# A hybrid decoder layer on one core: sliding-window units inside the input panels, operands stacked as high and low part

## The chip, the core and the metric

The kernel runs on one core of a Trainium2 chip. Its engines work side by side and meet only through semaphores: PE (TensorE) multiplies into PSUM, DVE (VectorE) and ACT (ScalarE) read PSUM and SBUF, POOL (GpSimd) reads SBUF, SP (SyncE) issues DMAs. Each engine runs its own instructions in program order. The metric is the device time of one execution in microseconds (us), lower is better.

## The reference, cut to what matters

One decoder layer, 512 tokens, width 2048, all in float32. A norm, one input projection whose columns feed two head groups, attention in both, an output projection, a norm, a gated FFN.

```python
proj = h @ w_in[layer]
c_q, c_kv, k_r, sq, sk, sv = jnp.split(proj, split_idx, axis=-1)   # 512, 512, 64, 1024, 128, 128
...
out_a = mla_attention(q, k_a, v_a)          # 8 heads, dense causal, latents c_q and c_kv
out_b = swa_attention(sq..., sk..., sv..., sinks[layer], rel_bias)
```

and of the sliding group, 16 heads of 64, in two groups of 8 that share a key and a value head:

```python
s = jnp.einsum('bnqhgd,bnkhd->bnhgqk', qb, kb) * scale     # 128 queries against 256 keys
s = jnp.where(valid, s + bias, NEG_INF)
m = jnp.maximum(jnp.max(s, axis=-1, keepdims=True), sink)
p = jnp.exp(s - m)
probs = p / (jnp.sum(p, axis=-1, keepdims=True) + jnp.exp(sink - m))
out = jnp.einsum('bnhgqk,bnkhd->bnqhgd', probs, vb)
```

## The kernel before

Every float32 product is made of three matmuls in the faster fp32r format: each operand is split into a high part (ACT's copy, rounded) and a low part (DVE's subtraction), and `three` (L722) sums high x high, high x low and low x high.

**Input panels.** The 1088 + 1280 columns of w_in are 19 panels of 128 columns, q = 0 to 18: four of c_kv, four of c_q, the rotary key, the sliding keys, the sliding values, and eight of sliding queries (q = 11 to 18). SP fetches a panel into `raw[q % 2]` (`fetch`, L733), 1 MB, when the low part of panel q-2 is written (`lo_ready`). ACT makes the high part of panel q+2 when PE has finished panel q (`used`), DVE the low part (`split_hi` L453, `split_lo` L465). PE runs 16 x 3 matmuls of 512 columns for a panel (L2426). DVE takes the result out of PSUM with the norm's factor (`take`, L1720; semaphore `taken`). ACT's and DVE's loops over the panels (L1122, L1710) hold, in this order for each q: units if there are any, the take, the splits for q+2.

**Sliding units.** A unit is one group of four heads (gh) and one block of 128 queries (n): 16 units, u = 4 gh + n. With n = 0 there is no earlier block of keys, so it has half the keys. A pipeline step `window(s)`, written once for each engine, holds: PE (L2377) the scores of unit s, the transposes of the probabilities of unit s-3, the values of unit s-4; DVE (L1669) bias and maxima of unit s (L1680), the reciprocal of s-1, the low half of the transposed probabilities of s-3 (L1698); ACT (L1083) the high half of s-3, the four exponentials of s (L1106), in their middle the copy of values s-4 to `mix_s` (L1091); POOL the scaling by the reciprocal (L974). Steps 0 and 1 stand in panel 17, steps 2 to 19 after the panels; the first product of the next stage (`rotary_queries`, `queries`) is woven into steps 17 to 19.

For the scores two heads of 64 lie on 128 partitions; the keys are padded with zeros (`kpad`) so that each of the two sees only its own 64 rows. A full unit has two `three` of 512 columns, one with n = 0 two of 256. For the values `vpad` is padded likewise, and a full unit has four `three` of 256 columns, one with n = 0 two.

**After the units.** Four pairs of dense heads. `keys_of`, `values_of`, `scores` (L2479 to L2516) of a pair need the split w_uq and w_ukv panels (q = 19, 20 and so on), and `keys_of` writes to bank 0 when DVE has copied the rotary queries from it (`r_in`, L1816). Then the output projection and the FFN, which fill the rest of the span.

The order on every engine is written out by hand in these loops.

## Time and profile before

| | |
|---|---|
| median of 3 runs | 1902.78 us (1902.52 to 1903.36) |
| the profiled execution | 1902.99 us |
| its span | 1901.2 us |
| PE busy | 1874.4 us |
| DVE busy | 1511.3 us |
| ACT busy | 915.2 us |
| POOL busy | 63.1 us |

The median is over runs without the profiler. The span is from the first to the last instruction of the profiled execution. Matmuls are pipelined: a record of one lasts longer than the distance to the next, so the time of a stream is read from starts. Times in the rows are from the span's start. An idle time that a row names is that of the engine just before the instruction, and the arrow says what ended it.

### The profile page before, as it was taken

The page shows a single profiled execution, that of the slowest core. Times are in us where ns is not written, and L with a number is a line of the kernel's source. Part 1 is how long each engine was busy: PE and PEld are TensorE (multiplying, and loading weights), DVE is VectorE, ACT ScalarE, POOL GpSimd, SP SyncE. Part 2 cuts the span into 40 slices and gives each one's busy share as a digit, 9 for nine tenths or more (in the row PEclk, how much of TensorE's full clock was granted, in tenths as well). Part 3 has the DMA queues.
Part 4 walks back from the last instruction along what each step waited for, and adds up shares of the span by engine and source line. Part 5 has one row for each costly group of instructions (what it writes and reads, how often), then busy time and mean ns, then how long its engine had stood idle before and what let it go on. Part 6 is the DMA issues. An engine that isn't in the chain of part 4 may idle for free.

```text
span 1901.2 us, 22151 instructions
## 1 busy us (share of the span) xinstructions
PE 1874.4 (99%) x8726; PEld 1556.3 (82%) x8726; DVE 1511.3 (79%) x1608; ACT 915.2 (48%) x1222; POOL 63.1 (3%) x63
## 2 busy tenths in 40 slices
PE   9999999999999999999999999999999999999998
PEld 7788788888888788888888888888888788888886
DVE  4863486775557988888888888889898988888888
ACT  5331484564465655454554554555455743333332
POOL 1210141000000000000000000000000000000000
PEclk9999999999999999999999999999999999999999
DMA  7444202137675437254272452734626865646563
GB/s 215 139 114 120 80 13 89 52 118 259 230 268 192 112 111 252 80 178 159 96 255 89 166 183 91 236 102 153 198 92 242 313 242 219 227 160 258 218 224 130
DMA packets 206197, 317.18 MB, mean 167 GB/s; under 512 B 9972, under 2 KB 143181, under 8 KB 199949
## 3 DMA queue, kind: packets, MB, share of 16 engines
q1 hardware_dynamic: 202128, 305.69, 47.1%
q10 hardware_dynamic: 3036, 6.66, 1.1%
q0 software_dynamic: 928, 3.41, 0.8%
q8 instruction: 69, 1.13, 0.2%
q14 instruction: 36, 0.29, 0.0%
HBM read 262.49 MB, written 52.98 MB: 166 GB/s over the span
## 4 chain that ended last, share of the span: by engine, by line
PE 61%; DVE 3%; issue 1%; DMA 1%; ACT 0%; DVEq 0%; ACTq 0%
PE pair L2664 13%; PE pair L2666 13%; PE pair L2665 13%; PE pair L2713 6%; PE pair L2714 6%; PE pair L2715 6%; PE pair L2675 1%; PE pair L2734 1%; PE pair L2732 1%; PE pair L2733 1%; DVE unit_lo L1923 1%; DMA w_b<-in_w_down 1%; DVE ring_lo L2172 0%; DMA h_forms<-h_stage 0%; ACT unit_hi L1339 0%
## 5 line engine op out<-in xcount | busy, mean ns | idle before, releaser
L2664 PE MATMUL pair<-unit_hi,xf_hi 128*128 128x512 f32 x1224 | 481.3, 393 | 6.6 <-DVE unit_lo L1923 6.6
L2666 PE MATMUL pair<-unit_hi,xf_lo 128*128 128x512 f32 x1224 | 476.9, 390 | 0.0
L2665 PE MATMUL pair<-unit_lo,xf_hi 128*128 128x512 f32 x1224 | 476.4, 389 | 0.0
L2664 PEld LDWEIGHTS pair<-unit_hi,xf_hi 128*128 128x128 f32 x1224 | 229.9, 188 | 55.5 <-issue 5.8
L2666 PEld LDWEIGHTS pair<-unit_hi,xf_lo 128*128 128x128 f32 x1224 | 229.8, 188 | 48.5
L2665 PEld LDWEIGHTS pair<-unit_lo,xf_hi 128*128 128x128 f32 x1224 | 230.0, 188 | 46.4
L469 DVE TENSOR_TENSOR wlo<-raw,whi 128x2048 fp32r<-128x2048 f32 (+2 forms) x59 | 124.1, 2110 | 93.1 <-ACT whi L462 93.0
L2713 PE MATMUL pair<-ring_hi,hfs 128*128 128x512 f32 x480 | 187.4, 390 | 1.5 <-ACT ht L1363 0.8
L2714 PE MATMUL pair<-ring_lo,hfs 128*128 128x512 f32 x480 | 186.8, 389 | 0.0
L2715 PE MATMUL pair<-ring_hi,hfs 128*128 128x512 f32 x480 | 186.8, 389 | 0.0
L462 ACT ACTIVATE whi<-raw 128x2048 fp32r<-128x2048 f32 (+2 forms) x60 | 105.0, 1757 | 146.2 <-PE pair L726 141.2
L1482 ACT ACTIVATE ring_hi<-w_b 128x2048 fp32r<-128x2048 f32 (+1 forms) x55 | 95.9, 1760 | 120.9 <-DVE w_b L2152 53.9
L2172 DVE TENSOR_TENSOR ring_lo<-w_b,ring_hi 128x2048 fp32r<-128x2048 f32 (+1 forms) x55 | 115.0, 2090 | 4.7 <-ACT ring_hi L1482 4.6
L724 PE MATMUL pair<-act_hi,whi 128*128 128x512 f32 x288 | 114.6, 398 | 3.1 <-DVE wlo L1606 2.3
L725 PE MATMUL pair<-act_lo,whi 128*128 128x512 f32 x288 | 112.2, 390 | 0.0
L726 PE MATMUL pair<-act_hi,wlo 128*128 128x512 f32 x288 | 112.2, 390 | 0.0
L2184 DVE TENSOR_TENSOR y<-y,pair 128x1024 f32<-128x1024 f32 x63 | 76.6, 1215 | 43.4 <-PE pair L2715 43.4
L2713 PEld LDWEIGHTS pair<-ring_hi,hfs 128*128 128x128 f32 x480 | 90.1, 188 | 21.7 <-DVE ring_lo L2172 2.2
L2715 PEld LDWEIGHTS pair<-ring_hi,hfs 128*128 128x128 f32 x480 | 90.1, 188 | 18.9
L2714 PEld LDWEIGHTS pair<-ring_lo,hfs 128*128 128x128 f32 x480 | 90.1, 188 | 18.5
L724 PE MATMUL pair<-whi,mixt 128*128 128x512 f32 x256 | 100.1, 391 | 0.1
L726 PE MATMUL pair<-whi,mixt 128*128 128x512 f32 x256 | 99.6, 389 | 0.0
(392 smaller groups left out, 3427.9 us busy)
## 6 DMA issues: line engine op xcount, KB each, us to landing
w_b<-in_w_down SPq DMA_DIRECT2D x40, 1024.0 KB, 5.1
h_forms<-h_stage SPq DMA_DIRECT2D x71, 512.0 KB, 4.9
raw<-in_w_o SPq DMA_DIRECT2D x32, 1024.0 KB, 5.0
hfs<-h_forms SPq DMA_DIRECT2D x30, 1024.0 KB, 8.1
raw<-in_w_in SPq DMA_DIRECT2D x16, 1024.0 KB, 6.0
w1a<-in_w_gate SPq DMA_DIRECT2D x16, 512.0 KB, 3.7
w1a<-in_w_up SPq DMA_DIRECT2D x16, 512.0 KB, 5.9
w1b<-in_w_gate SPq DMA_DIRECT2D x16, 512.0 KB, 3.9
```

Source lines behind the costliest of these rows:

```text
L462: last = nc.scalar.activation(dst, src, ACT.Copy)
L469: last = nc.vector.tensor_tensor(dst, src, f(hi), ALU.subtract)
L724: nc.tensor.matmul(out_ap, a[0], b[0], start=first, stop=False)
L725: nc.tensor.matmul(out_ap, a[0], b[1], start=False, stop=False)
L726: return nc.tensor.matmul(out_ap, a[1], b[0], start=False, stop=last)
L2172: nc.vector.tensor_tensor(ring(ring_lo, n), weights_form(f_, np_), f(ring(ring_hi, n)), ALU.subtract).then_inc(d_lo, 1)
L2664: nc.tensor.matmul(dst, a[0], w[0], start=(at, k) == (0, 0), stop=False)
L2665: nc.tensor.matmul(dst, a[0], w[1], start=False, stop=False)
L2666: last = nc.tensor.matmul(dst, a[1], w[0], start=False, stop=(at, k) == (3, 1))
L2713: nc.tensor.matmul(dst, a[0], b[0], start=k == 0, stop=False)
L2714: nc.tensor.matmul(dst, a[0], b[1], start=False, stop=False)
L2715: last = nc.tensor.matmul(dst, a[1], b[0], start=False, stop=k == np_ - 1)
```

## The change

- The sliding queries, keys and values are no longer padded. A query operand `sq_parts` holds for each head its high part on 64 partitions and its low part on the other 64; `sk_parts` holds the high part (and, in a second tile, the low part) of the keys on both halves. A unit's scores are, for each of its four heads, two matmuls of 256 columns (128 with n = 0) that contract over 128 partitions.
- The values are stacked along the output: `sv_parts` has 64 columns of high and 64 of low part, so a value matmul has 512 columns and its result has high x probabilities on partitions 0 to 63 and low x probabilities on 64 to 127. There are four such matmuls for a unit (two with n = 0). ACT copies the lower 64 partitions to `pv_low` and DVE adds both into `mix_s` (`value_add`), where ACT alone copied before. DVE does the addition of unit s-5 at the head of step s; the next unit's values wait for it (`s_out`).
- Steps 0 to 11 run inside panels 13 to 18, two in each: on PE after the 8th and the 14th of a panel's 16 chunks, on ACT and DVE at the head of the panel's turn. These steps use one pair of banks for scores, so the scores of s wait for the maxima of s-1. Steps 12 to 19 follow the panels.
- The queries are split panel by panel, as soon as a panel is taken, and only two panels of them are held.
- To make room, the low part of panels 12 to 20 is written over the raw panel (`low_part`, `in_place`), and the fetch of panel q then waits for `used` of panel q-2. The first w_uq panel comes in four pieces.
- Bank numbers, addresses, the place of the rotary key's parts and what the third w_o panel's fetch waits for change with it. POOL no longer zeroes `kpad` and `vpad`.

```diff
+        def in_place(q):
+            return Q_SQ + 1 <= q <= Q_UKV
+        def low_part(q):
+            return wlo_raw[q % 2] if in_place(q) else wlo[q % 2]
...
             def fetch(q, src, view):
-                if q >= 2:
+                if in_place(q - 2):
+                    sp_.wait_ge(used, q - 1)
+                elif q >= 2:
                     sp_.wait_ge(lo_ready, q - 1)
...
                 if i == 2:
-                    sp_.wait_ge(act_l, N_ROTATED)
+                    sp_.wait_ge(act_l, N_KG2)
...  (ACT)
+            def split_queries_hi(j):
+                act.wait_ge(taken, Q_SQ + j + 1)
+                if j >= 4:
+                    act.wait_ge(s_qk, 4 * (j // 2 - 1))
+                for e in range(2):
+                    rows = slice(64 * e, 64 * e + 64)
+                    last = nc.scalar.activation(sq_parts[j // 2 % 2][rows, 2 * (j % 2) + e, :], sq[j % 2][rows, :],
+                                                ACT.Copy)
+                last.then_inc(q_hi, 1)
...
                         act.wait_ge(s_pv, u + 1)
-                        nc.scalar.activation(mix_s[:, 2 * gh:2 * gh + 2, P * n:P * n + P],
-                                             bank[7][:, 0:256].rearrange("p (c n) -> p c n", c=2),
-                                             ACT.Copy).then_inc(s_out, 1)
+                        if u:
+                            act.wait_ge(s_out, u)
+                        nc.scalar.activation(pv_low[0:64, :], bank[7][64:128, :], ACT.Copy).then_inc(s_low, 1)
...
-                if q == N_IN - 2:
-                    window(0)
-                    window(1)
+                for s in panel_windows(q):
+                    window(s)
+                if what == "sq":
+                    split_queries_hi(j)
                 if 0 < q < N_IN - 1:
                     split_hi(q + 2, q % 2)
...  (DVE)
+            def value_add(u):
+                gh, _, n, _ = unit(u)
+                dve.wait_ge(s_low, u + 1)
+                for e in range(2):
+                    high, low = (t[0:64, 256 * e:256 * e + 256].rearrange("p (c n) -> p c n", c=2)
+                                 for t in (bank[7], pv_low))
+                    c0 = 2 * (gh % 2)
+                    last = nc.vector.tensor_tensor(mix_s[gh // 2][64 * e:64 * e + 64, c0:c0 + 2, P * n:P * n + P],
+                                                   high, low, ALU.add)
+                last.then_inc(s_out, 1)
...
             def window(s):
+                if s >= 5:
+                    value_add(s - 5)
...
-                    take(sq[:, j, :]).then_inc(taken, 1)
+                    take(sq[j % 2][:, :]).then_inc(taken, 1)
+                    split_queries_lo(j)
                 if 0 < q < N_IN - 1:
                     split_lo(q + 2, q % 2)
...
-            for s in range(2, UNITS + 3):
+            for s in range(FIRST_LATE, UNITS + 4):
                 window(s)
                 if s == UNITS + 1:
                     dve.wait_ge(ukv_hi, 1)
                     first_values_lo(0)
-            dve.wait_ge(hi_ready, Q_UKV + 1)
-            first_values_lo(1)
+                if s == UNITS + 2:
+                    dve.wait_ge(hi_ready, Q_UKV + 1)
+                    first_values_lo(1)
+            value_add(UNITS - 1)
...  (PE)
-                    if s == 1:
-                        pe.wait_ge(taken, N_IN - 2)
-                    if s >= 2:
-                        pe.wait_ge(s_max, s - 1)
+                    if s == FIRST_LATE:
+                        pe.wait_ge(taken, N_IN)
+                    elif s:
+                        pe.wait_ge(s_max, s if s < FIRST_LATE else s - 1)
                     keys = slice(P * n - P + lo, P * n + P)
-                    for cc in range(2):
-                        dst = bank[(s + 1) % 2 * 2 + cc].rearrange("p (e k) -> p e k", e=2)[:, :, lo:256]
-                        last = three(dst, [qs[gh % 2][i][:, cc, P * n:P * n + P] for i in range(2)],
-                                     [kpad[i][:, g, :, keys] for i in range(2)], True, True)
+                    for hd in range(4):
+                        dst = score_bank(s, hd).rearrange("p (e k) -> p e k", e=2)[:, hd % 2, lo:256]
+                        q_both = sq_parts[gh % 2][:, hd, P * n:P * n + P]
+                        nc.tensor.matmul(dst, q_both, sk_parts[0][:, g, keys], start=True, stop=False)
+                        last = nc.tensor.matmul(dst, q_both, sk_parts[1][:, g, keys], start=False, stop=True)
...
-                    parts = [(kb, e, h) for kb, h in halves(u) for e in range(2)]
-                    for m, (kb, e, h) in enumerate(parts):
+                    parts = [(kb, h, i) for kb, h in halves(u) for i in range(2)]
+                    for m, (kb, h, i) in enumerate(parts):
                         pe.wait_ge(s_lo, h + 1)
-                        c0 = 64 - 64 * e
-                        last = three(bank[7][:, 0:256], ...
+                        last = nc.tensor.matmul(bank[7], sv_parts[:, n - 1 + kb, g, :], spt[u % 2][i][:, kb, :],
+                                                start=m == 0, stop=m == len(parts) - 1)
...
-                    if q == N_IN - 2 and k == 7:
-                        window(1)
+                    if q >= Q_UNITS and k in (7, 13):
+                        window(panel_windows(q)[k // 13])
```

Here `Q_SQ` is 11, `Q_UNITS` 13, `Q_UKV` 20, `FIRST_LATE` 12.

## Rows read from the trace of the kernel before

**Rows 1.** The page, parts 1 and 2: busy time by engine; granted clock in 40 slices.

```profile
PE 1874.4 (99%) x8726; PEld 1556.3 (82%) x8726; DVE 1511.3 (79%) x1608; ACT 915.2 (48%) x1222; POOL 63.1 (3%) x63
...
PEclk9999999999999999999999999999999999999999
```

**Rows 2.** Windows: length; busy us of PE, PEld, DVE, ACT, POOL; clock; DMA share, GB/s.

```profile
159.15:227.89 68.74, 68.74 (x307) 57.03 (x306) 22.86 (x41) 18.16 (x30) 2.93 (x2) 1.00 0.34 92
227.89:276.62 48.73, 44.41 (x308) 39.45 (x307) 45.18 (x194) 44.30 (x164) 21.89 (x13) 1.00 0.12 33
276.62:290.92 14.30, 14.30 (x91) 12.71 (x90) 7.26 (x11) 6.17 (x14) 2.58 (x3) 1.00 0.04 3
```

**Rows 3.** Waits of PE, whole trace: us in total, times, longest.

```profile
PE pair L724 <- DVE wlo L1606: 2.3, 1, 2.3
...
PE pair L724 <- ACT mix_s L1091: 2.1, 5, 0.7
```

**Rows 4.** Timeline of PE: start us, us, line, out<-in, count.

```profile
236.14 1.03 PE L2407 MATMUL pair<-ident,sp 128*128 128x128 f32 x8
237.01 0.39 PE L724 MATMUL pair<-spt_hi,vpad_hi 128*128 128x256 f32 x1
237.23 0.28 PE L725 MATMUL pair<-spt_lo,vpad_hi 128*128 128x256 f32 x1
237.35 0.29 PE L726 MATMUL pair<-spt_hi,vpad_lo 128*128 128x256 f32 x1
```

**Rows 5.** Timeline of DVE and ACT behind panels 14 and 15.

```profile
181.11 0.69 DVE L1722 TENSOR_TENSOR sq<-pair,rrow 128x512 f32<-128x512 f32 x1 [6.58 <-PE pair L726]
...
191.99 0.69 DVE L1722 TENSOR_TENSOR sq<-pair,rrow 128x512 f32<-128x512 f32 x1 [6.58 <-PE pair L726]
...
192.05 1.92 ACT L462 ACTIVATE whi<-raw 128x2048 fp32r<-128x2048 f32 x1 [8.96 <-PE pair L726]
...
194.00 2.29 DVE L469 TENSOR_TENSOR wlo<-raw,whi 128x2048 fp32r<-128x2048 f32 x1 [1.32 <-ACT whi L462]
...
196.21 1.29 DVE L1661 TENSOR_TENSOR qs_lo<-sq,qs_hi 128x512 fp32r<-128x512 f32 x2
```

**Rows 6.** DMA issues from 165, 181 and 190 us: size, us from issue to landing.

```profile
raw<-in_w_in SPq DMA_DIRECT2D x1, 1024.0 KB, 5.7
...
raw<-in_w_in SPq DMA_DIRECT2D x1, 1024.0 KB, 6.9
...
raw<-in_w_uq SPq DMA_DIRECT2D x1, 768.0 KB, 4.7
```

**Rows 7.** Timeline of DVE among the units.

```profile
229.03 0.42 DVE L1680 CUSTOM_DVE_ANT_0 sp<-pair,bias 128x256 f32<-128x256 f32 x1
...
229.37 0.42 DVE L1680 CUSTOM_DVE_ANT_0 sp<-pair,bias 128x256 f32<-128x256 f32 x1
...
230.80 0.42 DVE L1680 CUSTOM_DVE_ANT_0 sp<-pair,bias 128x256 f32<-128x256 f32 x1
...
235.69 1.26 DVE L1698 TENSOR_TENSOR spt_lo<-pair,spt_hi 128x512 fp32r<-128x512 f32 x2
...
236.87 0.41 DVE L1680 CUSTOM_DVE_ANT_0 sp<-pair,bias 128x256 f32<-128x256 f32 x1
```

**Rows 8.** Timeline of DVE: four operations on 64 partitions.

```profile
131.58 2.78 DVE L1722 TENSOR_TENSOR skd<-pair,rrow 64x512 f32<-64x512 f32 x4
```

**Rows 9.** Timeline of ACT among the units.

```profile
227.15 1.15 ACT L1067 ACTIVATE qs_hi<-sq 128x512 fp32r<-128x512 f32 x2 [9.66 <-PE pair L726]
...
238.24 1.07 ACT L1081 ACTIVATE spt_hi<-pair 128x512 fp32r<-128x512 f32 x2
...
239.19 0.52 ACT L1106 ACTIVATE sp<-sp,st 128x256 f32<-128x256 f32 x1
...
240.18 0.38 ACT L1091 ACTIVATE mix_s<-pair 128x256 f32<-128x256 f32 x1
```

**Rows 10.** Timeline of DVE and PE before the keys.

```profile
289.44 0.69 DVE L1816 COPY t_sb<-pair 128x512 f32<-128x512 f32 x1
...
290.92 0.40 PE L724 MATMUL pair<-ckv_hi,whi 128*128 128x512 f32 x1
```

More of the change, by code:

```diff
@@ L67 @@
 Q_KR = [what for what, _, _ in IN_PANELS].index("kr")
+Q_SQ = [what for what, _, _ in IN_PANELS].index("sq")
+Q_UNITS = Q_SQ + 2
 PAIRS = MLA_HEADS // 2
@@ L137, in build @@
         wlo = [sb(f"wlo{i}", 32 + 8 * i, [P, 2048], F32R) for i in range(2)]
+        wlo_raw = [sb(f"wlo_raw{i}", 8 * i, [P, 2048], F32R) for i in range(2)]
         ident = sb("ident", 220, [P, P])
@@ L489, in half_bank @@
         def half_bank(h):
-            return bank[4 + h % 3]
+            return bank[4 + (h + 1) % 3]
         def value_bank(h):
@@ L754, in _ @@
                 q = Q_MLA + 2 * p
-                fetch(q, wuq_v[:, :, 384 * p:384 * p + 384], k4(raw[q % 2], 384))
+                if p == 0:
+                    first = k4(raw[q % 2], 384)
+                    for c0, w, a in ((192, 128, 128), (NOPE, ROPE, 256), (192 + NOPE, ROPE, 320), (0, 128, 0)):
+                        if a == 128:
+                            fetch(q, wuq_v[:, :, c0:c0 + w], first[:, :, a:a + w])
+                        else:
+                            sp_.dma_start(first[:, :, a:a + w], wuq_v[:, :, c0:c0 + w]).then_inc(uq_in, 16)
+                else:
+                    fetch(q, wuq_v[:, :, 384 * p:384 * p + 384], k4(raw[q % 2], 384))
                 fetch(q + 1, wukv_v[:, :, 512 * p:512 * p + 512], k4(raw[(q + 1) % 2]))
@@ L948, in _ @@
             pool.wait_ge(made, 7)
-            for t in (*kpad, vpad[0]):
-                make(nc.gpsimd.memset(f(t[:]), 0.0))
             for latent in range(2):
@@ L1153, in _ @@
                 if what == "sk":
-                    act.wait_ge(made, 11)
                     act.wait_ge(taken, q + 1)
-                    for i in range(4):
-                        g, e = i // 2, i % 2
-                        rows = slice(64 * e, 64 * e + 64)
-                        copy_hi(kpad[0][rows, g, e, :], skd[rows, g, :])
-                if q == N_IN - 4:
-                    act.wait_ge(taken, N_IN - 6)
-                    split_queries_hi(0, 0)
-                    split_queries_hi(0, 1)
+                    copy_hi(sk_parts[0][:, :, :], skd[:, :, :])
                 if what == "sv":
                     act.wait_ge(r_done, 1)
-                    copy_hi(kr[0][:, :], kr_a[:, :])
+                    copy_hi(kr[0][:, :], kraw[:, :])
                 if q == N_IN - 8:
                     act.wait_ge(sv_t, 1)
-                    copy_hi(vpad[0][:, :, :, 64:128], bank[4].rearrange("p (b g d) -> p b g d", b=TB, g=2))
+                    copy_hi(sv_parts[:, :, :, 0:64], bank[4].rearrange("p (b g d) -> p b g d", b=TB, g=2))
             act.wait_ge(used, N_IN)
-            load_band(1)
-            split_queries_hi(1, 0)
-            split_queries_hi(1, 1)
-            transposed_out(0)
-            for s in range(2, UNITS + 4):
+            for s in range(FIRST_LATE, UNITS + 4):
                 window(s)
@@ L1657, in latent_norm, with split_queries_lo @@
                     sub_lo((ckv, cq)[n][1][:, i, :], craw[n][:, i, :], (ckv, cq)[n][0][:, i, :])
-            def split_queries_lo(gh, half):
-                dve.wait_ge(q_hi, 2 * gh + half + 1)
-                nc.vector.tensor_tensor(qs[gh % 2][1][:, half, :], sq[:, 2 * gh + half, :],
-                                        f(qs[gh % 2][0][:, half, :]), ALU.subtract).then_inc(q_lo, 1)
+            def split_queries_lo(j):
+                dve.wait_ge(q_hi, j + 1)
+                for e in range(2):
+                    rows, other = slice(64 * e, 64 * e + 64), slice(64 - 64 * e, 128 - 64 * e)
+                    part = sq_parts[j // 2 % 2][:, 2 * (j % 2) + e, :]
+                    last = nc.vector.tensor_tensor(part[other, :], sq[j % 2][rows, :], f(part[rows, :]),
+                                                   ALU.subtract)
+                last.then_inc(q_lo, 1)
+            def value_add(u):
+                gh, _, n, _ = unit(u)
+                dve.wait_ge(s_low, u + 1)
+                for e in range(2):
+                    high, low = (t[0:64, 256 * e:256 * e + 256].rearrange("p (c n) -> p c n", c=2)
[4 more added lines that the diff above has]
+                last.then_inc(s_out, 1)
             def reciprocal_of(u):
@@ L1678, in window @@
                     for hd in range(4):
-                        scores = bank[(s + 1) % 2 * 2 + hd // 2].rearrange("p (e k) -> p e k", e=2)[:, hd % 2, lo:256]
+                        scores = score_bank(s, hd).rearrange("p (e k) -> p e k", e=2)[:, hd % 2, lo:256]
                         last = nc.vector.tensor_tensor_reduce(
@@ L2568, in out_products @@
                 last.then_inc(used, 1)
-            for s in range(2, UNITS + 4):
+            for s in range(FIRST_LATE, UNITS + 4):
                 if s == UNITS + 1:
```

119 lines of the change are left out of this document (53 added, 66 removed).

## The prediction, made before the changed kernel was seen

> **What bounds the kernel now.** I read the page first. PE is busy for 99% of the span and its granted clock is at the upper level, 2.4 GHz, in every slice [rows 1] (1.00 in the stretches of [rows 2]), so the end is moved only by PE: by matmuls taken out, or by waits put in or taken out. The profiled execution took 1902.99 us, 1.79 us more than its span, and lies 0.2 us above the median of 1902.78. I work against 1902.99.
>
> Then the stretches [rows 2]. Input panels 13 to 18 run from 159.15 to 227.89 with PE never idle: 68.74 us, in which units 0 and 1 compute their scores. The other units follow alone, 227.89 to 276.62, where DVE is busy for 45.2 of 48.7 us, ACT for 44.3 and PE idles for 4.3; its waits there are short, the five for ACT's copy of the values 0.7 us at most [rows 3]. The last units' values are mixed with the first query products until the keys start at 290.92. So panels plus units take 131.77 us. Outside the panels DVE and ACT are as full as PE; inside them they are nearly empty. What is moved goes from the one place to the other.
>
> **Unit costs.** The takes of two panels are 10.88 us apart [rows 5] and a panel has 48 matmuls of 512 columns: 0.227 us each. From start to start a matmul of 256 columns takes 0.119 us (0.12 in the rows) and eight transposes 0.87, so four some 0.4 [rows 4]. The change puts a unit after 24 of its matmuls (at 5.44 us) and another 18 later (4.08 more); 6 follow (1.36).
>
> **PE work removed.** A full unit had 6 score matmuls of 512 columns and 12 value matmuls of 256: 1.36 + 1.43. It gets 8 of 256 (0.95) and 4 of 512 (0.91): 0.93 us less. Units 0, 4, 8, 12 had 6 + 6 of 256 (1.43) and get 8 of 128 and 2 of 512. No row has such a matmul on split data with 128 columns. The nearest are the transposes at 0.10 us each, with the same 128x128 load; from above it is the 0.227 of 512 columns. I take 0.10: 0.80 + 0.45 = 1.25; the upper end adds 1.0 us per unit. Sum: 12 x 0.93 + 4 x 0.18 = 11.9 us. This is all that the change can earn in matmuls.
>
> **What replaces it in a panel.** From panel 12 on the low part is written over the raw panel, so the fetch of panel q+2 waits for `used`, the end of panel q, where it waited for an earlier low part. With panel q's end as zero, before: take at 0.2, high part on ACT, low part on DVE from 2.2 to 4.5 [rows 5]. After: issue at 0.2, landing 5.8 us later (the first two of [rows 6]: the eight such fetches from 111 to 186 us lie between 5.6 and 6.0, but for one of 6.9), ACT 1.95, DVE 2.2: 10.2 us. That is no trouble for the panel itself, which is due a panel later. But DVE and ACT run in program order (no row of them starts past one that waits [rows 5]), and the low part stands ahead of the next two units there. Ahead of it are also the take, ACT's query halves and DVE's, done by about 4.1 us, so the DMA ends last.
>
> PE reaches the first unit at 5.44. Its scores need nothing, its transposes nothing, at 7.26 it wants values(u), and that waits for `s_out` of u-1, which is now made by DVE's value_add at the head of its own unit: 10.2 + 0.77 + 0.1 = 11.1. The 0.77 is no row; two 256-element operations out of PSUM, priced from the 128x256 score operation (0.345 start to start, 0.42 the last) [rows 7]. Bounds: 0.42 for both, or 1.4 from the 64-partition takes of 512 [rows 8]. With this, panel by panel:
> - 13 (units 0, 1): the scores of 1 wait until unit 0's maxima free the one pair of banks, 10.2 + 1.25 = 11.5, PE is there at 10.3: wait 1.2, length 13.8.
> - 14 (2, 3): maxima of 2 at 12.0 against 10.5: wait 1.5, length 14.7.
> - 15 (4, 5): maxima, reciprocal, low half (1.2) and value_add(0): 13.95 against 13.46: wait 0.5, length 16.2.
> - 16 (6, 7): 11.1 against 7.26: wait 3.85, length 19.7.
> - 17 (8, 9): 11.1 against 7.1: wait 4.0, length 19.7.
> - 18 (10, 11): here the fetch before is w_uq in four pieces, 768 KB. As one it lands in 4.7 [rows 6]; as four between that and 5.8 plus three issues of 0.37. I take 5.2, which gives 9.5 against 7.26: wait 2.2, length 18.1.
>
> Second units of 16 to 18 wait for nothing: DVE is through with the first at 14.3, PE comes at 16. Sum 102.2 us, 13.3 of it waits, against 68.7: **33.5 more**.
>
> **The tail.** At panel 18's end (T) ACT is still in unit 11 for about 1.5 us, then two query halves (1.15 [rows 9]) and DVE's two (1.29 [rows 5]) must be done before unit 12 may start: T + 4.1, where before PE went straight on. From there the units alternate between DVE (value_add 0.77, maxima and what hangs on them 1.77, low halves 1.18 [rows 7], reciprocal 0.3) and ACT (transposed halves 0.95, four exponentials 2.0, the copy of the low values 0.5 to 0.6 [rows 9]): after the maxima ACT needs two exponentials and the copy (1.6) before DVE can add, so a unit takes about 4.05 us, on PE only 2.7. Followed operation by operation from T: scores of 12 at 4.1 (eight matmuls, 0.8), maxima of 12 done at 6.1, value_add(8) at 8.45 (ACT's copy is late, at 7.7), maxima of 13 at 10.1, value_add(9) at 12.5, then every 4.05 us: 10 at 16.5, 11 at 20.6, and 0.1 + 0.45 for the values of 12: the first query product starts at 21.2, 17.1 us after the scores of 12 (16.2 before). That product to the keys: 3 x 2.72, transposes 1.74, values 2.73 make 12.7. Two waits come in. values(15) needs value_add(14), which stands on DVE behind the second half of the w_ukv split, in turn behind ACT's copy: 0.95. And the keys need `r_in`, the copy of bank 0, which DVE began 1.5 us ahead [rows 10] and now makes after value_add(15): ACT 0.2 + 0.57, DVE 0.77 + 0.69: 2.25 after the last value matmul. Together 16.1 (14.3 before). T to keys: 4.1 + 17.1 + 16.1 = 37.3 against 63.0: **25.7 less**.
>
> **Small edits.** Handovers between short and long matmuls cost some 0.1 us each (0.22 between the first two value matmuls where 0.12 is usual [rows 4]), eight more of them inside panels: 0.8. The smaller key splits, the zeroing that GpSimd no longer does and the kept rotary key lie beside panels in which PE never idles: nothing. Fetch 21 now waits for the second query product; landing in 4.7 us [rows 6] it comes before its splits are wanted, since the keys are held up by `r_in`: nothing, and about 1.1 us if that wait were not there. Fetch 22 has 3 us of slack. The third w_o panel waits for mix chunks 8 to 11, some 5 us later than before, and is split 8 us after its new landing: nothing.
>
> **Sum:** 33.5 - 25.7 + 0.8 = +8.6. 1902.99 + 8.6 = **1911.6 us**. Its own bounds: landing 5.6 to 6.9 (-1 to +5), value_add 0.42 to 1.4 (-2 to +5, not both in full), 128 columns (+1.4, the rest vanishes in waits), the chain around T (+-1.5): 1907 to 1916.
>
> **Rivals.** *Faster, the panel hides it.* The place is the wait of the first unit's values. It decides at the point where landing, split and value_add take under 7.3 us, so a landing within 2 us. Then the 13.3 us of waits go: 1898.3. For it: the DMA engines are only about a third busy there [rows 2]. Against it: eight fetches of 1 MB, none under 5.6. Chance 0.10.
> *No change, the tail runs at PE's pace.* If DVE and ACT overlap better over the four late units than my chain has it, their 17.1 us fall towards PE's own 10.4: 6.7 less, 1904.9. For it: before, with both nearly full, a unit took 3.7. Against it: DVE's own operations sum to 4.0. Chance 0.15.
> *Slower still, the clock falls.* The longest idle of PE that the trace shows between two busy stretches is 2.3 us [rows 3], and the granted clock stays at its upper level [rows 1]. The new waits of 3.85, 4.0 and 4.1 are longer than any. If the lower level (1.2 GHz) followed each for as long as the wait itself, matmuls of 0.227 would take 0.45 and each would cost 2 us: 1917.6. The Trainium skill, page "TensorE: Matmul & The Clock Gate", section "Why this matters for your kernels", warns that idle gaps between bursts of matmuls send the clock back to its half rate; by that rule this rival would be the likely one. No row here shows a drop after an idle. Chance 0.13.
> The forecast keeps 0.62.
>
> **Chances.** About 0.2% (3.8 us) is what this kernel's measurement can tell from no change. Faster: the first rival, 0.10. Same: the second and the forecast's lowest edge, 0.17. Slower: 0.73. The range 1903.5 to 1918 takes in all but the first rival and the far edges; about 0.17 is left out.
>
> **What would show it.** Right: panels 16 and 17 near 19.7 us each, PE idle some 4 us ahead of the value matmuls with DVE's addition as releaser; raw fetches issued at panel ends; an idle of 4 us ahead of unit 12; the keys released by the bank copy. Wrong: panels of 16 us, fetches issued early, or units near 3 us in the tail. A PE clock under 1.00 after those waits would speak for the third rival.

## The result, and the profile after

The changed kernel takes 1928.84 us (median of 4 runs, 1927.88 to 1932.41) against 1902.69 us of the kernel before on the same chip: ratio 1.0138, 95% interval 1.0126 to 1.0150. The forecast was 1911.6 us in a range of 1903.5 to 1918: the sign was right, the size was not, and the time lies outside the range by 11 us. The profiled execution took 1927.88 us, its span 1926.1.

The page of the changed kernel, parts 1 and 2 (answers to [rows 1]):

```profile
PE 1877.6 (97%) x8646; PEld 1555.3 (81%) x8646; DVE 1526.3 (79%) x1644; ACT 926.5 (48%) x1226; POOL 57.1 (3%) x59
...
PEclk9999988999999999999999999999999999999999
```

80 matmuls are gone and PE is busy for longer all the same. Two slices of its granted clock stand at 8, where before all forty stood at 9.

Windows of the changed kernel (columns as in [rows 2]): panels 13 to 18, from there to the first query product, to the keys, the 16 us behind the keys, the rest:

```profile
159.18:270.65 111.47, 97.31 (x473) 80.87 (x471) 61.55 (x195) 55.08 (x143) 16.69 (x11) 0.94 0.24 64
270.65:295.50 24.85, 15.60 (x86) 13.87 (x86) 18.69 (x71) 18.09 (x58) 8.33 (x5) 0.86 0.12 43
295.50:313.57 18.07, 14.76 (x66) 11.56 (x64) 10.21 (x18) 8.23 (x14) 1.90 (x1) 0.88 0.14 44
313.57:330.00 16.43, 16.43 (x85) 14.46 (x86) 9.65 (x19) 4.51 (x7) 3.42 (x8) 0.82 0.07 17
330.00:1926.00 1596.00, 1578.58 (x7234) 1307.73 (x7232) 1325.74 (x1225) 775.76 (x935) 7.82 (x14) 1.00 0.51 178
```

Panels: 111.5 us against 68.7. Panel 18's end to the keys: 42.9 against 63.0. From 330 us on the clock is 1.00 and nothing is lost. The keys start at 313.57 against 290.92 [rows 10], which is 22.65 of the 24.9 us by which the spans differ. The other 2.25 are a net: the keys' own product, up to the first matmul of 256 columns, takes 8.4 us against 5.5 before (2.9 lost, at a granted clock of 0.82), and 0.7 come back further on.

PE's waits in the changed kernel (us in total, times, longest; answers to [rows 3]). `mix_s` is what value_add writes, `sq_parts` the split queries, `st` the maxima (semaphore `s_max`), `t_sb` the copy of the rotary queries:

```profile
PE pair L2450 <- DVE mix_s L1700: 17.0, 8, 5.1
...
PE pair L2425 <- DVE sq_parts L1689: 4.4, 1, 4.4
PE pair L2425 <- DVE st L1728: 2.9, 3, 1.3
PE pair L750 <- DVE t_sb L1847: 2.4, 1, 2.4
```

The largest group is the waits for value_add. The longest of them, in panel 17, on PE's timeline, and on ACT's and DVE's:

```profile
233.13 1.06 PE L2439 MATMUL pair<-ident,sp 128*128 128x128 f32 x8
239.32 0.79 PE L2450 MATMUL pair<-spt_hi,sv_parts 128*128 128x512 f32 x1 [5.13 <-DVE mix_s L1700]
239.91 0.63 PE L2450 MATMUL pair<-spt_lo,sv_parts 128*128 128x512 f32 x1
240.34 0.63 PE L750 MATMUL pair<-act_hi,whi 128*128 128x512 f32 x1
240.76 0.63 PE L751 MATMUL pair<-act_lo,whi 128*128 128x512 f32 x1
...
244.79 0.39 PE L752 MATMUL pair<-act_hi,wlo_raw 128*128 128x512 f32 x1
245.02 0.39 PE L750 MATMUL pair<-act_hi,whi 128*128 128x512 f32 x1
```

```profile
234.28 1.91 ACT L478 ACTIVATE whi<-raw 128x2048 fp32r<-128x2048 f32 x1 [4.32 <-DMA raw<-in_w_in]
```

```profile
236.22 2.29 DVE L485 TENSOR_TENSOR wlo_raw<-raw,whi 128x2048 fp32r<-128x2048 f32 x1 [4.84 <-ACT whi L478]
238.43 0.84 DVE L1700 TENSOR_TENSOR mix_s<-pair,pv_low 64x256 f32<-64x256 f32 x2
```

The chain is the one that was forecast: landing, high part, low part, value_add, values. Two things weren't. The raw panel lands 7.2 us after its issue, not 5.8, and behind the wait the matmuls of 512 columns start 0.43 us apart instead of 0.23. Windows of 5 us around each long wait (the third number from the end is the granted clock; all windows between 155 and 330 us that are not shown have 1.00):

```profile
215.00:220.00 5.00, 3.59 (x10) 2.90 (x11) 4.74 (x18) 1.91 (x6) 1.39 (x1) 0.72 0.01 3
220.00:225.00 5.00, 5.00 (x27) 4.27 (x27) 1.33 (x5) 1.05 (x6) 0.51 (x1) 0.94 0.00 0
235.00:240.00 5.00, 0.68 (x2) 0.59 (x3) 3.74 (x10) 2.27 (x3) 0.00 (x0) 0.77 0.00 0
240.00:245.00 5.00, 5.00 (x14) 3.91 (x13) 2.72 (x12) 2.34 (x10) 1.90 (x1) 0.55 0.00 0
260.00:265.00 5.00, 4.79 (x14) 3.83 (x15) 4.21 (x17) 2.77 (x10) 1.90 (x1) 0.66 0.01 2
275.00:280.00 5.00, 4.77 (x20) 4.58 (x21) 3.59 (x17) 1.61 (x5) 1.07 (x1) 0.52 0.03 12
280.00:285.00 5.00, 5.00 (x33) 4.83 (x33) 4.04 (x17) 4.33 (x16) 1.62 (x2) 0.79 0.01 3
295.00:300.00 5.00, 5.00 (x16) 3.90 (x17) 2.37 (x6) 1.76 (x4) 1.90 (x1) 0.66 0.00 0
310.00:315.00 5.00, 2.62 (x8) 1.83 (x9) 2.72 (x5) 2.68 (x5) 1.29 (x3) 0.78 0.59 172
315.00:320.00 5.00, 5.00 (x14) 3.92 (x13) 2.23 (x3) 1.17 (x3) 2.13 (x6) 0.54 0.18 41
```

The clock fell to its lower level six times: behind the waits of 3.54, 5.13 and 2.27 us in panels 16 to 18, behind the 4.41 us at unit 12, behind two of 1.73 and 2.24 us in a row among the last units, and behind the 2.38 us ahead of the keys. One minus the clock, times the window, sums to 15.4 us: no more than that can be lost to the clock directly, and part of it lies inside the waits, where it costs nothing.

### The profile page after: what moved, and what is told of

It reads as the page before. It is cut to its first block, busy times and chain, and to the rows that moved or that the text cites. A ratio compares the mean times of both kernels' runs of the same rounds, so it can differ in the third digit from the quotient of the medians.

```text
span 1926.1 us, 22050 instructions
## 1 busy us (share of the span) xinstructions
PE 1877.6 (97%) x8646; PEld 1555.3 (81%) x8646; DVE 1526.3 (79%) x1644; ACT 926.5 (48%) x1226; POOL 57.1 (3%) x59
## 4 chain that ended last, share of the span: by engine, by line
PE 62%; DVE 2%; issue 1%; DMA 1%; ACT 0%; DVEq 0%; ACTq 0%
PE pair L2691 14%; PE pair L2693 13%; PE pair L2692 13%; PE pair L2740 6%; PE pair L2741 6%; PE pair L2742 6%; PE pair L2702 1%; PE pair L2759 1%; PE pair L2760 1%; PE pair L2761 1%; DMA w_b<-in_w_down 1%; DVE ring_lo L2203 0%; DVE unit_lo L1954 0%; DVE xf_lo L1948 0%; DVE w2a L1983 0%
## 5 line engine op out<-in xcount | busy, mean ns | idle before, releaser
L485 DVE TENSOR_TENSOR wlo<-raw,whi 128x2048 fp32r<-128x2048 f32 (+2 forms) x50 | 106.4, 2132 | 84.5 <-ACT whi L478 84.5
L478 ACT ACTIVATE whi<-raw 128x2048 fp32r<-128x2048 f32 (+3 forms) x59 | 104.8, 1782 | 120.4 <-PE pair L752 94.2
L751 PE MATMUL pair<-wlo,mixt 128*128 128x512 f32 x256 | 99.6, 389 | 0.0
```

The costliest lines, as they stand in the source:

```text
L478: last = nc.scalar.activation(dst, src, ACT.Copy)
L485: last = nc.vector.tensor_tensor(dst, src, f(hi), ALU.subtract)
L751: nc.tensor.matmul(out_ap, a[0], b[1], start=False, stop=False)
```

## The experiments

The hypothesis after these readings: most of the 17 us of excess is the clock's fall (the third rival's mechanism, far more than its 6 us), the rest the slower landings and the late units. The rival to it: the clock in the records is only a sign of idleness, and the waits cost what they cost. Under both, a second question: are the waits in the panels a matter of bandwidth and of the units' own chain, or only of the order in which DVE and ACT take their work?

**e_warm: dummy products in the waits.**

```diff
+            def warm(b, count):
+                for _ in range(count):
+                    nc.tensor.matmul(bank[b], cq[0][:, 0, 0:P], cq[0][:, 0, :], start=True, stop=True)
...
+                    if s in (6, 8, 10):
+                        q = Q_UNITS + s // 2
+                        pe.wait_ge(taken, q)
+                        warm((q + 1) % 2, {6: 14, 8: 20, 10: 8}[s])
                     if u >= 1:
                         pe.wait_ge(s_out, u)
```

> The changed kernel with dummy TensorE products (128x512 fp32r, 0.227 us each) put into its six longest waits, which they fill but are too few to outlast: 14, 20 and 8 ahead of the value products of units 2, 4 and 6 (the waits of 3.54, 5.13 and 2.27 us for value_add), 16 ahead of the scores of unit 12 (4.4 us), 6 and 9 ahead of the value products of units 11 and 12 (1.7 and 2.2 us), 9 ahead of the keys (2.4 us). Nothing that the kernel needs comes sooner. Theory: most of the 16.3 us by which the changed kernel is above the forecast is the granted clock, which falls behind those waits; then it stays at 1.00 in every 5-us window between 210 and 325 us, the panels and keys come some 12 to 15 us sooner in all, and the time is 1913 to 1917 us. Rival: the excess is the longer waits and landings themselves, and the clock in the records is without weight; then the time stays within 2 us of 1928.8.

Measured: 1917.0 us (1915.92 to 1920.11), ratio to before 1.0075 (1.006 to 1.009). Windows of e_warm around the same places, which come sooner by the time won; all others between 210 and 330 us have 1.00 too:

```profile
215.00:220.00 5.00, 4.66 (x21) 3.54 (x20) 4.74 (x18) 1.81 (x6) 1.30 (x1) 1.00 0.00 0
220.00:225.00 5.00, 5.00 (x29) 4.35 (x28) 2.87 (x15) 2.09 (x9) 0.60 (x2) 1.00 0.00 0
...
240.00:245.00 5.00, 5.00 (x32) 4.44 (x31) 2.68 (x11) 2.17 (x8) 1.35 (x1) 1.00 0.00 0
...
290.00:295.00 5.00, 5.00 (x28) 4.23 (x27) 3.02 (x6) 2.63 (x4) 0.47 (x1) 1.00 0.02 3
```

82 matmuls were added, and the kernel became 11.8 us faster. No work comes sooner for their sake: the fetches of panels 14, 15 and 16, each issued at a panel's end, are 13.8 and 14.7 us apart in e_warm, 13.8 and 14.9 in the changed kernel, and panel 15 lasts 17.6 us in both; panel 16, the first with a fall, lasts 19.8 us in e_warm and 21.4 in the changed kernel. That is the price of the clock, and the first hypothesis stands: the rival had the time within 2 us of 1928.8. What is left, 1917.0 - 1911.6 = 5.4 us, are the terms of the sum (below).

**e_warm3: only the three longest waits filled** (the same edit without the fillers of 8, 6, 9 and 9).

> e_warm with the dummy products in the three longest waits alone (3.54, 5.13 and 4.4 us: units 2 and 4's values, unit 12's scores); the waits of 2.3, 1.7 and 2.2 in a row, and 2.4 us stay open. Theory: the clock falls behind waits of 2.2 to 2.4 us too, though not each time; about 8 to 9 of the 11.8 us that e_warm brought come from the three long ones, and the time is 1919 to 1921 us with a spread of some 3 us between runs. Rival: only the long waits lower the clock, and what falls behind the short ones is their after-effect; then the time is e_warm's 1917 within 1 us.

Measured: 1921.16 us (1919.05 to 1923.25). Of the 11.8 us, 7.7 come from the three waits of 3.5 us and more, 4.2 from the shorter ones. The split is rough: the runs of e_warm and e_warm3 overlap (up to 1920.11, from 1919.05). In its profiled execution a wait of 2.36 us left the clock alone and the 1.73 and 2.24 us in a row did not:

```profile
258.47 0.50 PE L2461 MATMUL pair<-spt_hi,sv_parts 128*128 128x512 f32 x1 [2.36 <-DVE mix_s L1700]
...
285.71 0.50 PE L2461 MATMUL pair<-spt_hi,sv_parts 128*128 128x512 f32 x1 [1.73 <-DVE mix_s L1700]
290.01 0.50 PE L2461 MATMUL pair<-spt_hi,sv_parts 128*128 128x512 f32 x1 [2.24 <-DVE mix_s L1700]
```

```profile
260.00:265.00 5.00, 5.00 (x30) 4.38 (x29) 2.79 (x9) 2.77 (x10) 1.90 (x1) 1.00 0.00 2
...
290.00:295.00 5.00, 4.99 (x15) 3.89 (x16) 2.37 (x6) 1.84 (x5) 1.90 (x1) 0.66 0.01 3
```

In the changed kernel's own profile the wait of 2.27 us in the same place was followed by 0.66. The pair of 1.73 and 2.24 us isn't sure to lower it either: in e_late_split, e_keys and e_add_order (below) it left the clock at 1.00. So a wait of that length lowers the clock in some executions and not in others, which may be part of why the changed kernel's four runs differ by 4.5 us.

The start of the kernel shows it best, since PE's first products and this wait are the same in every version. Up to some 10.4 us PE waits 2.3 us for a low part, in all fourteen traces. The changed kernel and, below, e_warm3:

```profile
10.51 0.50 PE L750 MATMUL pair<-act_hi,whi 128*128 128x512 f32 x1 [2.31 <-DVE wlo L1631]
10.00:15.00 5.00, 4.49 (x22) 3.74 (x23) 2.91 (x4) 1.70 (x3) 0.00 (x0) 1.00 1.13 341
```

```profile
6.07 1.97 PE L2352 MATMUL pair<-ident,xin 128*128 128x128 f32 x16 [0.34 <-DMA xin<-in_x]
10.35 0.50 PE L750 MATMUL pair<-act_hi,whi 128*128 128x512 f32 x1 [2.32 <-DVE wlo L1631]
10.00:15.00 5.00, 4.65 (x13) 3.68 (x14) 2.75 (x4) 1.20 (x2) 0.00 (x0) 0.66 1.12 342
```

In nine traces, the kernel before among them, the clock stays at 1.00 behind this wait; in five (e_warm3, e_add_tail, e_fill12, e_best5, e_best6) it is 0.66 over the window, and the fetch that marks the start of panel 13 comes at 160.8 to 161.0 us, in the other changed versions at 159.2 to 159.7. The same five are those in which PE had gone through its first products sooner (eight of 128 columns in 1.16 us, in the others 1.5 to 2.1) and then waited 0.3 to 0.6 us for a load of x. What decides it isn't shown. It belongs to the execution and not to the version, so profiled executions can differ by 1.5 us for this alone, and 1.3 of the 5.6 us between the spans of e_warm3 and e_warm are of this kind.

**e_band: the bias load one window later.**

```diff
-                    if n == 3 and gh + 2 < 4:
-                        load_band(gh + 2)
+                    if n == 0 and 1 <= gh < 3:
+                        load_band(gh + 1)
```

> The changed kernel, with the loads of the bias tables for groups 2 and 3 issued one window later than before, so that they don't fly together with a raw panel. Theory: the raw landings of 7.2 us in panels 15 and 17 are two loads on one set of DMA engines; they become 5.8 us, and the wait of 5.13 us at unit 4's values in panel 17 becomes 3.7; one run of 1926 to 1928 us. Rival: the 7.2 us has another cause; landing and wait stay.

Measured: one run, 1925.78 us. DMA issues of panel 17 in the changed kernel, and below in e_band (KB, us from issue to landing):

```profile
raw<-in_w_in SPq DMA_DIRECT2D x1, 1024.0 KB, 7.2
bias<-bias_all ACTq DMA_DIRECT2D x1, 512.0 KB, 6.1
```

```profile
raw<-in_w_in SPq DMA_DIRECT2D x1, 1024.0 KB, 5.8
```

The wait in panel 17 fell from 5.13 to 3.72 us, and panel 15 lasts 16.2 us in place of 17.6. Both landings of 7.2 us were two loads in flight at once; the raw panel of panel 15 lands in 5.8 us too.

**e_add_tail: value_add at the end of its window.**

```diff
-                if s >= 5:
-                    value_add(s - 5)
                 if s < UNITS:
...
                                                 f(spt[u % 2][0][:, kb, :]), ALU.subtract).then_inc(s_lo, 1)
+                if s >= 4:
+                    value_add(s - 4)
```

> The changed kernel, with value_add(s-4) at the tail of VectorE's window(s) instead of value_add(s-5) at the head of the next one, so that it doesn't stand behind the wait for the raw panel and the panel's low part. Theory: the waits of the first window in panels 16, 17 and 18 (3.54, 5.13, 2.27 us for mix_s, 10.9 in all) are the add's place in VectorE's order alone; they go, and about 1 us comes back in each panel as a wait of the second window's scores for s_max, whose reduction stands behind the low part as before; with no wait over 2 us left in the panels the clock stays at 1.00 there (6.8 us of it). Time 1928.8 - 10.9 + 3 - 6.8 = 1914 us. Rival: the low part (2.3 us, at the end of a 7.2 us landing) holds the second window too, so that the reduction and transposed low part give the same waits one window later; then the time is within 4 us of 1928.8.

Measured: 1912.03 us (1910.68 to 1914.79), ratio 1.0048 (1.0033 to 1.0063). PE's waits for mix_s fell from 17.0 to 6.7 us, of which none over 0.6 is in a panel; those for s_max rose from 2.9 to 4.2. The place of an operation of 0.84 us in its queue is worth 16.8 us in the medians. The parts come from the profiled executions: 8.2 us of waits, net, and by the same sum over 5-us windows (6.8 us here, 15.4 in the changed kernel) 8.6 of clock. That they sum to the medians' difference is chance: these two executions are 13.1 us apart, since this one lost 1.5 us to the clock at its start and another 1.5 behind 330 us.

**e_late_split: the split of the next panel between the two windows.**

```diff
                 for s in panel_windows(q):
                     window(s)
+                    if s % 2 == 0 and s:
+                        split_lo(q + 1, (q + 1) % 2)
...
-                if 0 < q < N_IN - 1:
+                if 0 < q < Q_UNITS:
                     split_lo(q + 2, q % 2)
```

(and the same for ACT's split_hi)

> The changed kernel, with the split of the next but one panel (ScalarE's high part with its wait for the raw panel, VectorE's low part) moved from ahead of the first window to between the two windows of panels 14 to 18, where its panel is still half a panel away. value_add stays where it is. Theory: what holds TensorE in panels 13 to 18 is only that both windows stand behind the landing of a raw panel on the two in-order queues; moved, the waits of 1.3, 0.85, 3.54, 5.13 and 2.27 us go (13 us), the clock falls behind them too (6.8 us), and the time is 1908 to 1911 us; the wait at unit 12 and the keys stay. Rival: the two windows' own chain (reduction, exponentials, low part, add) is longer than half a panel, so that the second window waits 2 to 3 us in each of five panels in place of the first; then 1918 to 1925 us.

Measured: 1916.89 us (1914.43 to 1919.23), between the theory and its rival. The waits in front of the first windows went, and came back in front of the second ones, since value_add still headed its window and now stood behind the split there (panel 16, DVE and PE in e_late_split):

```profile
219.63 2.29 DVE L485 TENSOR_TENSOR wlo_raw<-raw,whi 128x2048 fp32r<-128x2048 f32 x1 [3.00 <-ACT whi L478]
221.84 0.84 DVE L1702 TENSOR_TENSOR mix_s<-pair,pv_low 64x256 f32<-64x256 f32 x2
```

```profile
222.73 0.50 PE L2454 MATMUL pair<-spt_hi,sv_parts 128*128 128x512 f32 x1 [2.17 <-DVE mix_s L1702]
```

Four such waits, of 1.2 to 2.2 us. I had asked what the moved step no longer delays, and not what it delays in its new place.

**e_keys: the rotary copy ahead of the last additions.** On DVE rotary_in(0) moves from behind value_add(15) to just behind window 18.

> The changed kernel, with the copy of the rotary queries (t_sb, 0.69 us) moved on VectorE from behind the last two value_adds to just behind window 18. Theory: the keys' wait of 2.38 us (for t_sb) goes, and with it the clock fall behind it (0.54 to 0.78 over 310 to 320 us, 3.3 us): 1928.8 - 5.5 = 1923.3 us. Rival: the keys then wait for the last value's copies or the low part of the first keys all the same, and the time is within 2 us of 1928.8.

Measured: 1923.5 us (1922.04 to 1926.34), ratio 1.0108 (1.0093 to 1.0123). The wait of 2.38 us is gone, the clock is 1.00 from there on, and the gain of 5.3 us is more than twice the wait. The profiled executions alone wouldn't show that: of their 5.5 us, 2.35 were won ahead of the moved copy, where the clock happened to stay up behind waits of 2.25 and 2.22 us, 4.9 around the keys, and 1.7 were lost again behind 330 us. But the changed kernel's own rows give the same price, 2.38 us of wait and fourteen matmuls that take 6.1 us where 0.227 each make 3.2:

```profile
313.57 0.76 PE L750 MATMUL pair<-ckv_hi,whi 128*128 128x512 f32 x1 [2.38 <-DVE t_sb L1847]
315.41 0.63 PE L751 MATMUL pair<-ckv_lo,whi 128*128 128x512 f32 x1
315.84 0.63 PE L752 MATMUL pair<-ckv_hi,wlo_raw 128*128 128x512 f32 x1
```

**e_add_order: e_add_tail, and on PE unit 9's transposes and unit 8's values ahead of unit 12's scores.**

> e_add_tail, and on TensorE unit 9's transposes and unit 8's value products (0.8 and 0.9 us) ahead of unit 12's scores. Theory: unit 12's scores wait for the last panel's queries (take, high part, low part) and for nothing that TensorE has to do; its wait falls from 5.08 us to 3.4, the time to 1910 us. If the granted clock falls only behind waits that are long enough, it may stay at 1.00 at 265 to 275 us, and the time is 1907.

Measured: one run, 1909.88 us. The wait at unit 12 fell from 5.08 to 2.71 us, not to 3.4: besides the 1.7 us of work drawn into it, PE now waits 0.76 us ahead of unit 8's values, for an addition. The clock fell behind the wait at unit 12 all the same (0.67 over 5 us).

**e_combo: e_add_tail, e_late_split, e_keys, e_band and the order of e_add_order together.**

> The changed kernel with five moves in the queues' order together: value_add at the tail of its window (as in e_add_tail), the split of the next panel between the two windows (as in e_late_split), the rotary copy ahead of the last adds (as in e_keys), the bias load one window later, so that it doesn't fly with a raw panel, and on TensorE unit 9's transposes and unit 8's values ahead of unit 12's scores. Theory (all that is lost is the order of two in-order queues, and the clock behind waits of over 2 us): e_add_tail's 1912.0, less 5.4 for the keys and their clock, less 1.7 for the work drawn into unit 12's wait, less 2 to 3 of the 5.4 us of waits that e_add_tail leaves in the panels: 1902 to 1903 us, no difference to the kernel before that can be told. Rival (the moves overlap, the units' own chain of reduction, exponentials, low part and add bounds the panels whatever the order): 1906 to 1909 us.

Measured: 1908.47 us (1907.11 to 1909.07), ratio 1.0026 (1.0016 to 1.0037): the rival's case. The moves overlap. The panels' waits fell from the 5.4 us that e_add_tail leaves to 3.8 only: with the additions out of its way the later split saves the waits for s_max, and it brings others (1.2 us for a low part that is now late at the start of panel 15, 0.6 and 1.3 for the next group's queries), and 1.5 us for an addition ahead of unit 8's values. Unit 12 still waits 2.7 us, with the clock at 0.50 over the next 5 us.

**e_fill12: e_combo with the rotary query product in the wait at unit 12.** PE computes rotary_queries(0) ahead of unit 12's scores; these take banks 2 and 3, unit 13's banks 0 and 1.

> e_combo, and the rotary queries' products (12 matmuls, 2.7 us) moved from ahead of unit 14's transposes to ahead of unit 12's scores, where TensorE waits for the last panel's queries; unit 12's scores take banks 2 and 3 and unit 13's banks 0 and 1, so that the rotary product has bank 0. Theory: the wait of some 3.3 us that is left at unit 12 in e_combo nearly goes, and so does the clock fall behind it (3.4 us): 1902.5 - 2.7 - 3.4 = 1896 to 1897 us, faster than the kernel before by 0.3%. Rival: taken out of the late units, the rotary product no longer covers unit 14's chain there, and a wait of 2 to 3 us comes up between units 13 and 15 in its place; then within 2 us of e_combo.

Measured: 1906.98 us (1904.88 to 1909.29). Of the 6.1 us expected, 1.5 came. The wait at unit 12 went (2.71 us), but two of 0.6 and 0.7 us came up at unit 13 and one of 1.9 at the first scores of the keys in place of 1.25, and the last units' 1.73 and 2.24 us stayed, with the clock at 0.56 and 0.76 over the ten us behind them. The rival, in the larger part.

**e_best4 and e_best5.** Splits where the changed kernel has them; the additions, bias load, unit 12's order and rotary product as above; queries(0, 0) ahead of unit 11's values, queries(0, 1) ahead of window 17. e_best5 has the second window of panels 13 to 17 behind the last K chunk (`k in (7, 15)` for `(7, 13)`).

> Without the move of the splits (they stand where the changed kernel has them): value_add at its window's tail, the bias load one window later, unit 9's transposes and unit 8's values and then the rotary queries' product (bank 0) ahead of unit 12's scores, its copy right behind the last panel's queries on VectorE; the query products of the two heads, which stood ahead of windows 18 and 19, ahead of unit 11's values (bank 1) and ahead of window 17 (bank 2), the scores of units 12, 14 and 15 in banks 2 and 3. Theory: each filler stands where TensorE waits on VectorE's 4.3 us a unit (1.7 us there, 2.2 one unit later) or on the last units' chain, so from e_add_order's 1909.9 the keys' wait and clock (4.1), unit 12's wait and clock (4.4) and 3 to 4 us of the last units go: 1898 to 1900 us. Rival: the last units are bound by their own chain (values, low copy, add: 2.6 us a unit, four in a row), and what filled it before now leaves it open: 1903 to 1906 us.

> e_best4 with the second window of panels 13 to 17 behind the last K chunk instead of behind the fourteenth, so that the two windows lie 5.5 us of products apart in place of 4.1. Theory: the waits of 0.9, 1.2, 0.9 and 0.9 us for s_max in panels 13, 14, 15 and 17 are the chain raw panel, low part, reduction, 5.2 us from the first window; they go, 3 to 4 us together: 1895 to 1897 us. Rival: the panel's end is what VectorE's take waits for, and the second window ahead of it on VectorE delays take, split and the next landing chain by as much: within 1 us of e_best4.

Measured: 1902.7 us (1901.87 to 1903.51), ratio 0.9997 (0.9988 to 1.0006), and 1902.13 us (1899.76 to 1902.5), ratio 0.9991 (0.9982 to 1.0000). They are 3.7 and 6 us above the middle of what was expected; e_best4 is level with the kernel before. The gain that is missing is in the last units: in e_best5 the values of units 14 and 15 go at 283.26 and 286.48, after waits of 1.45 and 2.01 us with a fall of the clock behind them, as in e_best4. e_best5 removed the panels' waits for s_max, as expected, and won 0.6 us by it, not 3 to 4: in e_best4 only 1.9 us of them were left, and the later windows brought 0.64 and 1.02 us of waits for the queries' low parts.

**e_best6: e_best5 with the w_ukv halves split in idle time.** The first half's high and low part behind window 16 instead of in and behind window 17, the second half's high part ahead of the low copy in window 18; first windows of panels 13 to 17 one chunk later.

> e_best5 with the first half of the key and value weights' split (high part on ScalarE, low part on VectorE, 1.06 and 1.23 us) moved from window 17 to behind window 16, where both queues are idle for 2 us, the second half's high part from behind window 18 into it, and the first windows of panels 13 to 17 one K chunk later. Theory: the waits of 1.45 and 2.01 us for the adds of units 13 and 14 are these halves standing ahead of the low copy and of unit 15's low part; the first goes, the second falls by half, the clock's fall behind them (1.7 us in e_best5's records) with them, and 0.6 to 1.0 us of the waits of 0.64 and 1.02 us for the queries' low part: 1902.1 - 2.0 - 1.5 - 0.8 = 1898 us, 0.25% faster than the kernel before. Rival: each idle of VectorE there is the shadow of the last units' own chain, and the halves push it; then within 1 us of 1902.

Measured: **1897.8 us** (1896.12 to 1899.38, 9 runs) against 1902.45, ratio 0.9971 (0.9962 to 0.9981): faster than both kernels. Its windows over panels 13 to 18, from there to the keys, and the stretch behind the panels where the clock still falls (waits of 0.69 and 1.56 us stand ahead of it):

```profile
160.80:251.46 90.66, 90.33 (x473) 76.90 (x472) 61.74 (x195) 55.69 (x143) 16.70 (x11) 1.00 0.30 79
251.46:285.53 34.07, 27.40 (x149) 21.44 (x148) 27.84 (x86) 24.65 (x68) 12.16 (x10) 0.98 0.20 62
...
285.00:290.00 5.00, 5.00 (x17) 3.88 (x17) 3.36 (x6) 3.57 (x6) 1.12 (x4) 0.71 0.01 3
```

The same 473 matmuls (as the records have them) that took 111.5 us take 90.7, with 0.3 us of PE idle. Panels to keys is 124.7 us, against 131.8 before [rows 2] and 154.4 in the changed kernel. Of the 7 us against before 4.7 reach the median. In this execution, 4.1 us shorter in span than that before, 1.65 were lost ahead of the panels, which start at 160.80 instead of 159.15: it is one of the five whose clock fell behind the wait at 10.4 us. The rest went by the clock behind the keys' start.

## Why the prediction was right and wrong

**What bounds it, and the sign: right.** PE at its pace before, and waits put in by the change: the releasers are those forecast (value_add, the maxima, the queries' low part, the rotary copy), at the places forecast.

**The panels' waits: the steps right, one size off.** By panel, forecast 1.2, 1.5, 0.5, 3.85, 4.0, 2.2 us; measured 0.75, 1.30, 1.16 (0.85 and 0.31), 3.54, 5.13, 2.27. In e_warm, at the upper clock throughout, panels 13 to 18 lasted 13.8, 14.7, 17.6, 19.8, 21.3, 18.6 us against 13.8, 14.7, 16.2, 19.7, 19.7, 18.1. The term that was mis-sized is "landing 5.8 us": right for panels 13, 14 and 16, 7.2 in 15 and 17, where load_band issues 512 KB from ACT at the same time. The diff says where that load is issued, and [rows 6] had one of 6.9; I took it for scatter and kept it for the bounds. Price 3.0 us (1.4 and 1.6 in these two panels); e_band shows the cause for the landing and for the wait, and its panel 15 lasts the 16.2 us that were forecast.

**The tail: right in its parts, 2.4 us short.** Unit 12's scores came 4.6 us behind panel 18's end (forecast 4.1); in e_warm the keys start 39.7 us behind it, against 37.3. The late units took 4.31 us each, not 4.05 (285.71 to 290.01 in e_warm3's rows above is the last of three such steps). The bound named was ACT's copy behind two exponentials; for two of the three steps it was DVE alone, whose operations leave no gap there, with value_add at 0.84 and not 0.77; only in the last did it wait 0.71 us for that copy. The keys' wait was 2.38 (2.25 forecast).

**The clock: this step failed.** The third rival had the mechanism: granted clock under 1.00 behind the new waits. It had it for three waits, at 2 us each, with a chance of 0.13, and was no part of the sum. e_warm puts 11.8 us on it, of which e_warm3 gives 7.7 to the three waits of 3.5 us and more (2.6 each) and 4.2 to the shorter ones. Two errors. The price was a guess of the form "as long as the wait itself" where no row had a fall; in panel 17 the slow matmuls went on from 239.3 to about 244.2, at 0.43 instead of 0.23 us each: some 2.3 us, near the guess of 2. So for the long waits the size was nearly right, and what was missing is that three more places cost too. And the chance was set by an absence: that before's longest idle, 2.3 us, left the clock at 1.00 says nothing on idles of 4 and 5 us. It wasn't even true of that idle in general: it is the wait at 10.4 us, and the clock fell behind it in five traces of fourteen. The Trainium skill, page "TensorE: Matmul & The Clock Gate", section "Why this matters for your kernels", warned of a fall behind idle gaps. The traces agree (0.55 over the five us behind the wait of 5.13, 0.52 behind that of 4.41), and it should have been the likeliest case, with the forecast as its rival. With e_warm's price the sum is 1911.6 + 11.8 = 1923.4 us, and with the two landings (3.0) and the tail (2.4) 1928.8, which is what was measured. The 11.8 are themselves a difference to e_warm, so what this tests is the other part: the landings and the tail are the 5.4 us by which e_warm lies above the forecast.

**The other rivals.** "Faster, the panel hides it" needed a landing within 2 us; no raw panel of the changed kernel landed in under 5.7. Yet its place was well named: the panels' waits, 14.2 us as measured, can go by order and not by a faster load (5.4 left in e_add_tail, 0.3 in e_best6). "No change, the tail runs at PE's pace": it does not; 4.31 us a unit.

**Small edits: right as far as can be seen.** The forecast had 0.8 us for them in the panels, 103.0 in all; with the 3.0 of the landings that is 106.0, and e_warm's panels sum to 105.8. The 2.9 us lost behind the keys' start go with a clock of 0.82 there. From 330 us on 0.7 us came back in the changed kernel, and 1.7 were lost in e_keys' execution: shifts of that size, which no run here explains, bound what can be said of small terms.

What stays open: why a wait of some 2.3 us lowers the clock in one execution and not in the next (the one at 10.4 us in five of fourteen), and whether the landing of 6.9 us in [rows 6], with no bias load beside it, has a cause of its own.

## What to carry to other kernels

Moving dense work under other dense work pays what it removes only if the queues beside it are in the right order: here 31 us lay between the worst and the best order tried of the same operations, the clock's falls included. Look in each in-order queue for the step that waits for a transfer, and for small steps that stand behind it although somebody else waits for them; then look for what the moved step will delay in its new place. And when a change opens waits on an engine that hardly idled, price the clock's fall with the wait: a wait of 2.4 us cost 5.3 in this kernel. An idle that left the clock alone in one trace is no proof that it always does.

## What the runs showed of the hardware

- TensorE's granted clock fell to 1.2 GHz behind each wait of 3.5 us and more, in every profile that had one, and behind waits of 2.2 to 2.4 us in some (0.66 behind 2.27 us in the changed kernel, 1.00 behind 2.25 in e_keys and 2.36 in e_warm3; 0.66 behind the wait of 2.3 us at 10.4 us in five traces, 1.00 in nine). In e_best6 it was 0.71 behind waits of 0.69 and 1.56 us that ended 2.8 us apart. Products that nobody reads, put into the waits, kept it up: 82 matmuls more, 11.8 us less.
- Two loads from different queues at once stretch each other: 1 MB landed in 7.2 us beside 512 KB in 6.1, and in e_band, apart, they took 5.8 and 3.8 us.
- Matmuls on split data with 128 columns start 0.11 us apart (258.26 to 258.82 in e_best5, five in 0.56 us), with 256 columns 0.12, with 512 0.23.
